# A hybrid decoder step on one core: activations turned by VectorE, the first expert's rows picked on TensorE, the turns for the end split

## The reference, cut to what matters

```python
def moe_ffn(h, comb, wg, wu, wd):
    out = jnp.zeros_like(h)
    for e in range(N_EXPERTS):
        ye = (jax.nn.silu(h @ wg[e]) * (h @ wu[e])) @ wd[e]
        out = out + comb[:, e:e + 1].astype(h.dtype) * ye
    return out
```

## Time and profile before

| | us |
|---|---|
| median of 3 runs | 1032.35 (1032.21 to 1035.29) |
| the profiled execution | 1030.09 |
| its span, first to last instruction | 1028.1 |

### The profile page before, as it was taken

How to read it: one execution, slowest core, us unless ns; L and a number is a source line. 1 busy time by engine, 2 the same in 40 slices (tenths; PEclk the granted TensorE clock), 3 DMA queues, 4 the chain that set the end, 5 groups by cost and what they waited for, 6 DMA issues and landing times.

```text
span 1028.1 us, 20300 instructions
## 1 busy us (share of the span) xinstructions
PE 985.4 (96%) x8539; PEld 745.2 (72%) x8539; DVE 385.5 (37%) x853; ACT 235.2 (23%) x467; POOL 139.8 (14%) x230
## 2 busy tenths in 40 slices
PE   5999999999999999999999999997899999999995
PEld 2667666666666666666666677665889999999981
DVE  3121234677257986656540611226110100101016
ACT  2240122233363322242251300002320111101013
POOL 0000132342020443224300000000100000000010
PEclk8999999999999999999999999998999999999998
DMA  9853344564355555646542633432839999999984
GB/s 378 318 213 121 125 164 144 193 231 174 136 201 202 217 208 198 234 156 227 185 143 85 255 123 123 164 117 77 313 140 385 398 410 400 416 386 420 395 335 131
DMA packets 47155, 237.62 MB, mean 231 GB/s; under 512 B 6800, under 2 KB 11248, under 8 KB 23792
## 3 DMA queue, kind: packets, MB, share of 16 engines
q1 hardware_dynamic: 45120, 230.85, 59.9%
q0 software_dynamic: 1520, 5.34, 1.5%
q10 hardware_dynamic: 448, 0.50, 0.2%
HBM read 212.31 MB, written 24.36 MB: 230 GB/s over the span
## 4 chain that ended last, share of the span: by engine, by line
PE 90%; DVE 4%; ACT 2%; DMA 1%; issue 1%; POOL 1%; DVEq 0%; SPq 0%; ACTq 0%; POOLq 0%
PE pjB L827 16%; PE pjA L827 15%; PE states L1364 11%; PE pjA L1212 7%; PE pjB L1212 7%; PE states L1367 5%; PE pjB L1364 3%; PE pjA L1364 3%; PE states L836 2%; PE pjA L1367 1%; PE pjB L1367 1%; PE bank L1176 1%; PE bank L951 1%; PE states L1191 1%; PE states L951 1%
## 5 line engine op out<-in xcount | busy, mean ns | idle before, releaser
L827 PE MATMUL pjB<-hF,ring 128*128 128x320 f32 x608 | 173.5, 439 | 0.0
L827 PE MATMUL pjA<-hF,ring 128*128 128x320 f32 x608 | 171.9, 436 | 0.5 <-ACT regA L1610 0.5
L1367 PE MATMUL states<-ring,oF 128*32 128x384 f32 x1392 | 154.6, 491 | 0.0
L1364 PE MATMUL states<-ring,oF 128*32 128x128 f32 x1392 | 154.4, 273 | 0.0
L1364 PEld LDWEIGHTS states<-ring,oF 128*32 128x32 f32 x1392 | 151.9, 110 | 0.2 <-issue 0.2
L827 PEld LDWEIGHTS pjB<-hF,ring 128*128 128x128 f32 x608 | 114.4, 192 | 49.2 <-issue 5.9
L827 PEld LDWEIGHTS pjA<-hF,ring 128*128 128x128 f32 x608 | 113.3, 190 | 50.5 <-issue 7.0
L2606 DVE TENSOR_TENSOR oF<-oF,states 128x384 f32<-128x384 f32 x15 | 8.3, 554 | 151.1 <-PE states L1367 151.1
L2336 DVE TENSOR_TENSOR G<-G 128x320 f32<-128x320 f32 x32 | 48.8, 1562 | 0.0
L1948 POOL TENSOR_TENSOR G<-regA,G 128x128 f32<-128x128 f32 (+1 forms) x32 | 19.0, 593 | 196.8 <-ACT G L1666 196.8
L1367 PE MATMUL pjB<-ring,hF 128*32 128x384 f32 x360 | 42.2, 493 | 0.0
(11 more groups left out here) (508 smaller groups left out, 1418.8 us busy)
## 6 DMA issues: line engine op xcount, KB each, us to landing
ring<-in_w SPq DMA_DIRECT2D x171, 1024.0 KB, 8.1
G<-in_ss SPq DMA_DIRECT2D x16, 512.0 KB, 4.0
out_ss_new<-G SPq DMA_DIRECT2D x16, 512.0 KB, 2.7
G<-csd SPq DMA_DIRECT2D x16, 320.0 KB, 3.4
G<-in_sg SPq DMA_DIRECT2D x4, 1024.0 KB, 6.3
out_sg_new<-G SPq DMA_DIRECT2D x16, 256.0 KB, 2.9
yd<-hF SPq DMA_DIRECT2D x14, 288.0 KB, 6.4
rF<-in_w SPq DMA_DIRECT2D x2, 1024.0 KB, 9.9
```

The costliest lines, as they stand in the source:

```text
L827: mm = pe.matmul(pj[g % 2][:, 0:T], w[:, k, half * P:half * P + P], hF[:, k, :], start=(k == 0), stop=(k == KT - 1))
L1364: pe.matmul(bank[CAP:P, c * P:(c + 1) * P], rows(c, True), w[:, WIDE:512], start=first and c == 0, stop=last, tile_position=(0, CAP), skip ...
L1367: mm = pe.matmul(bank[QUAD * c:QUAD * c + QUAD, 0:WIDE], rows(c, False), w[:, 0:WIDE], start=first, stop=last, tile_position=(0, QUAD * c) ...
```

## The change

Three things are changed in the fast path.

The activations of experts 0 to 14 are turned by VectorE: 16 transposes of 32 partitions by three blocks of 32 x 32, instead of three turns on TensorE and a copy. The last expert keeps `turn_act`.

The first expert's rows no longer come through memory. VectorE builds a selection `selE` (a 1 where a token's rank in expert 0 is the row's), six matmuls pick the rows out of `hT`, ACT and VectorE copy them to `rowsE`, eight turns bring them into `heF`, and `gate_up(0)` reads that. The three steps that lead to `meta` are made before the turn additions, and the scan `iota` before the ranks. SP's third load waits until the selection has read `hT`, which it overwrites. All five blocks of sorted rows are turned after `gate_up(0)`.

Of the twelve turns for the end, 0 to 5 stay in the dispatch (three ahead of the selection, two behind it, one behind the eight turns), on other banks; 6 to 11 are made between the token blocks, and the turn of `selS` behind them. The blocks of sorted rows alternate between two pairs of banks, so that a block waits for the copy of the last but one.

```diff
@@ SyncE
                 sp.dma_start(xs01[:, 1, :], d["xd"][P:2 * P, :]).then_inc(s_xe[1], 16)
+                sp.wait_ge(s_oss, GH + 1)
                 sp.dma_start(hT, d["xd"][2 * P:XROWS, :].rearrange("(a p) c -> p a c", p=P)).then_inc(s_xe[1], 16)
@@ TensorE
-            for n in range(12):
-                if n >= 4:
-                    pe.wait_ge(s_tmc, n - 3)
-                bank = (b[4], b[5], pj[0], pj[1])[n % 4]
+            tm_bank = [b[2], b[2], b[2], b[2], b[4], b[5]] + [b[4], b[5]] * 3
+            def turn_late(n):
+                if n in (4, 5):
+                    pe.wait_ge(s_htc, 6)
+                elif n:
+                    pe.wait_ge(s_tmc, n if n < 4 else n - 1)
...
+            for n in range(3):
+                turn_late(n)
+            pe.wait_ge(s_dsp, DISPATCH_FIRST)
             for t, (c0, c1, rows) in enumerate(TT):
+                pe.wait_ge(s_htc, 2 * t + 2)
+                for h in range(2):
+                    mm = pe.matmul((b[3], b[0])[h][0:CAP, :], selE[0:rows, t, :], hT[0:rows, t, 512 * h:512 * h + 512],
+                                   start=(t == 0), stop=(t == 2))
+            mm.then_inc(s_oss, 1)
+            turn_late(3)
+            turn_late(4)
+            pe.wait_ge(s_rqc, 4)
+            for k in range(KT):
+                mm = pe.transpose(pj[k // 4][:, k % 4 * CAP:(k % 4 + 1) * CAP], rowsE[:, k * P:k * P + P], ident[0:CAP, 0:CAP])
+            mm.then_inc(s_oss, 1)
+            turn_late(5)
 
             def turn_tokens(t):
                 pe.wait_ge(s_xe[0] if t == 0 else s_xe[1], 32 if t == 0 else 48)
-                if t:
-                    pe.wait_ge(s_htc, 6 + t)
-                    pe.wait_ge(s_hev, t)
+                if t >= 2:
+                    pe.wait_ge(s_htc, 6 + t - 1)
+                    pe.wait_ge(s_hev, t - 1)
...
-                he = heS[:, :, 0:CAP] if isinstance(e, int) and e == 0 else heF[:, v]
+                he = heF[:, v]
...
                     mm.then_inc(s_used, 1)
-                    if turn and h == 0:
-                        turn_act(turn[0])
...
                     if isinstance(e, int) and e == 0:
-                        for t in range(1, XROWS // P):
+                        for t in range(XROWS // P):
                             turn_tokens(t)
-                        turn_act(0)
+                            turn_late(TM_EARLY + t)
+                        turn_late(11)
+                        turn_picks()
+                        pe.wait_ge(s_htc, 6 + XROWS // P)
@@ ScalarE
+            for n in range(3):
+                copy_late(n)
+            act.wait_ge(s_oss, GH + 1)
+            act.activation(rowsE[:, 0:512], b[3][0:CAP, :], ACT.Copy).then_inc(s_rqc, 1)
+            copy_late(3)
+            copy_late(4)
+            act.wait_ge(s_oss, GH + 2)
+            act.activation(heF[:, 0, 0:4, :], pj[0][:, 0:4 * CAP].rearrange("p (k c) -> p k c", c=CAP), ACT.Copy).then_inc(s_rqc, 1)
+            copy_late(5)
...
-                        copy_tokens(1)
+                        for t in range(2):
+                            copy_tokens(t)
+                            copy_late(TM_EARLY + t)
                         act.wait_ge(s_htc, 8)
                         act.wait_ge(s_hev, 2)
                         rows_of(0, 1, 0)
                         for t in range(2, XROWS // P):
                             copy_tokens(t)
+                            copy_late(TM_EARLY + t)
+                        copy_late(11)
@@ VectorE
+            dve.tensor_tensor_scan(iota, ones[:, 0:CAP], ones[:, 0:CAP], 0.0, ALU.mult, ALU.add).then_inc(s_cmb, 1)
             dve.wait_ge(s_rank, 1)
...
+            dstep(dve.tensor_copy(rFst, ranks[:, :, 0]))
+            dve.wait_ge(s_cmb, 1)
+            for t in range(3):
+                ds_(dve.tensor_scalar(selE[:, t, :], iota, rFst[:, t:t + 1], os_[:, t, 0:1], ALU.is_equal, ALU.mult))
+            assert ds_.n == DISPATCH_FIRST, ds_.n
             dve.wait_ge(s_rta, 7)
             for n, (t, half) in enumerate(TURNS):
...
+                if j == 0:
+                    dve.wait_ge(s_oss, GH + 1)
+                    dve.tensor_copy(rowsE[:, 512:D], b[0][0:CAP, :]).then_inc(s_rqc, 1)
...
+            dve.wait_ge(s_oss, GH + 2)
+            dve.tensor_copy(heF[:, 0, 4:8, :], pj[1][:, 0:4 * CAP].rearrange("p (k c) -> p k c", c=CAP)).then_inc(s_rqc, 1)
...
                 def turned(e, v):
-                    dve.wait_ge(s_rd, GH + PAIRS + 1 + e)
+                    dve.wait_ge(s_eac, e + 1)
                     if not (isinstance(e, int) and e < 2):
                         moe_used(dve, e, 5, 2)
+                    for q in range(4):
+                        to = slice(QUAD * q, QUAD * q + QUAD)
+                        for c in range(4):
+                            at = slice(QUAD * c, QUAD * c + QUAD)
+                            rows = slice(QUAD * c, QUAD * c + QUAD) if c < BLOCKS else slice(CAP, P)
+                            ins = dve.transpose(actT[to, v, :, rows],
+                                                actE[at, :].rearrange("p (k f) -> p k f", f=P)[:, :, QUAD * q:QUAD * q + QUAD])
+                    ins.then_inc(s_hev, 1)
```

## The result

| | before | after |
|---|---|---|
| median (runs beside each other) | 1032.28 us (1028.69 to 1035.29, 4 runs) | 1016.61 us (1015.88 to 1017.40, 4 runs) |
| the profiled execution | 1030.09 | 1015.97 |
| its span | 1028.1 | 1014.2 |

The ratio is 0.985, 95% interval 0.9817 to 0.9883: the changed kernel is faster, by 1.2 to 1.8%. The span fell by 13.9 us, the median by 15.7.

A forecast was written before the change was run, and what follows sets the result against it. TensorE bounded the kernel, with transfers keeping its pace and nothing over. Of 13.9 us saved on TensorE, 3.2 + 3.75 = 6.9 would come through: 1030.09 - 6.9 = 1023.2, plus 2.26 gives 1025.5 us, range 1018 to 1030.

The forecast's parts named there:

- the transfers can't follow: Expert stage: 15.74 us an expert would need 425 GB/s, the stream ran at about 400; gain 6.9 us, not 13.9.
- The share of 0.98 to 1.01: DMA engines' share in the windows of one expert, read as no room to spare.
- always full: Weight stream from the third expert: no tile lands in 5.0 us again, so it ends only 3.2 us earlier.
- 221.0 us for 13.2 experts: Weight tiles and y writes from 778.7 to 999.7, read as the transfers' limit of 16.8 us an expert.
- rival 1: Expert stage: the transfers follow and TensorE stays the bound; gain 13.9, 1018.5 us, from 16.0 us an expert; chance 0.17.
- 2.26 us between profiled run and median: Whole kernel: the runs' median lies 2.26 above the profiled run, added to 1023.2 to give 1025.5 us.
- 2.4 + 11.5 = 13.9 us: TensorE's path alone: 2.4 from the second expert's earlier start, 11.5 from turns dropped in experts 1 to 14.
- Token block and late turns: Between the first and second expert: five tokens, late turns, picks and a copy wait, 10.7 us instead of 7.5.
- 726.9 forecast: Front: `gate_up(0)` starts near 726.9 instead of 732.8, a gain of 5.9 us at full clock.
- rival 2: Front: clock falls, four of six selections take twice their time; gain 3.8, 1028.6 us; chance 0.15.
- The third load: SP's load in the front: issued near 730.6, lands near 739.5 instead of 737.3, hardly holding up the token blocks.
- The cover of 15.7 us: Experts' VectorE turns: `down(e)` comes 5.25 + 10.5 = 15.7 us later, less some 1 us, hiding 4.3 us of transposes.

The follow-up runs named there:

- filled kernel: The kernel before with 16 more TensorE turns while it waits for the first rows from memory: 1030.14 us against 1032.8, ratio 0.9977.
- twenty turns: The changed kernel with twenty more identity turns on TensorE in every expert, between the halves of down: 18.40 us an expert.

## Why the prediction was wrong, point by point

**The failed step** is "but the transfers can't follow", from which 13.9 us became 6.9. Its three readings were right as rows and wrong as a limit.
- The share of 0.98 to 1.01: it is 0.94 at 364 GB/s with 2.59 us of room, 1.02 at the limit, and 1.02 at 336 GB/s in a dip of the kernel before. It tells that something is always under way, not that nothing more would go through.
- No tile lands after 5.0 us again, so "always full": landing times of mostly 8 to 9.5 us went with 0.76 us of room, at the limit they are 13.2.
- 221.0 us for 13.2 experts: tiles were issued from 770.6 to 988.6, 218.0 us or 16.56 an expert. That is TensorE's 16.57, and the rest of the 16.8 is the longer landing of the last tile. 6.685 MB in 16.57 us are 403 GB/s. The rate of about 400 was TensorE's pace read off the transfers, no second witness. The window of 420 GB/s in the same rows showed that more was possible; it was given to rival 1, with 0.17.

By the prediction's own condition ("decides from 16.0 us an expert") the measured 15.81 makes it rival 1: 1018.5 us.

**The second mis-sized term** is the 2.26 us between profiled run and median, carried over unchanged. After it is 0.64. As far as the filled kernel and the mean clocks tell, before's median held a fallen clock at the first expert, which the profile happened not to show; the new front has no wait for rows from memory, and in all twelve profiles with it the clock is 1.00 there. This made the median's gain 15.7 where the span's is 13.9.

**What held.** By TensorE alone 2.4 + 11.5 = 13.9 us; measured 2.8 to the second expert and 14.0 to the last weights. The transposes: 0.27 us taken, 0.270 measured. Token block and late turns: 10.7 taken, 9.9 measured (738.13 to 748.06). `gate_up(0)`: 726.9 forecast, 727.31, from two errors that nearly cancel. The additions came at 715.84 instead of 716.8 (the ranks were ready 0.3 us earlier, and the steps put in behind them took 1.5 us instead of 2.2), and the first two selections ran at half clock, 3.2 us to the third instead of 1.76, as rival 2 had it for four of six. The third load held nothing up, and y went unharmed.

**A slip that cost little.** The cover of 15.7 us is not every expert's. `last` runs `down(14)` straight behind `down(13)`, so expert 14 has 5.25 us for 1 + 4.3: this is the 0.2 us wait for L2687 in the list above, and the 9.3 us with three times the transposes.

## What to carry to other kernels

A rate measured while another engine sets the pace is that engine's pace: divide the bytes by its period first, and if the rate comes out, nothing is known of the limit but that it is no lower than the best window. To find the limit, leave out some of the pacing engine's work and keep the bytes; two such runs settled here what three readings of the trace had wrong. Windows much shorter than the period help as well: in the trace of the kernel before they show 426 GB/s for 6 us on end. And where TensorE waits for a round trip, look at the granted clock of more than one execution: the profiled one may be the lucky one.

## What was not expected of the hardware

- With room, the transfers don't slow down evenly: they run at 426 GB/s and dip about once an expert (336 and 267 GB/s in the windows above), in the kernel before with tiles queued and a DMA share of 1.02. Why is open.
- The limit of this mixed stream is steady, 422 to 423 GB/s in every window; the paced one scattered from 372 to 420. Scatter between equal windows can be a sign of room, but room can be there without it: with twenty turns six windows lie between 362 and 366.
- The same wait of 1.7 us before the same four records at the end had three outcomes in thirteen profiles: they took 1.93 us in six (the clock stayed at 1.00 until they were done), 2.21 to 2.56 in four (it fell to 0.50 late among them) and 3.15 to 3.39 in three (it fell near their start).
- The shortened changed kernel, with a quarter of the experts' TensorE work gone, is only 7.5 us shorter in its span (1006.7). Both limits now lie within 0.1 us an expert of each other, so more TensorE time saved there buys little unless bytes go as well.
